# One more pair of convolution taps moved into the attention stage, and a projection that waits for its two operand halves one by one

## What is computed

```
a = rmsnorm(h, g);  z = a @ w_in                    # split into SGU, conv and MLA columns
y_a = spatial gating unit(z_sgu)
y_b = conv module(z_conv):  a * sigmoid(g), causal depthwise convolution of 31 taps over tokens
      (256 channels), layernorm, silu, 256x256 product
y_c = latent attention(c_q, c_kv, k_pe):  8 heads, causal, q and k of 96, v of 64
h  += [norm(y_a) | norm(y_b) | norm(y_c)] @ w_o
h  += two-level mixture of experts(rmsnorm(h))
h  += sigmoid(rmsnorm(h) @ W_g) * rmsnorm(p @ W_p)
```

## Time and profile before

| | |
|---|---|
| three executions | 2377.6, 2371.58, 2376.19 us; median 2376.19 |
| the profiled execution | 2380.11 us, span 2378.4 us from first to last instruction |
| mean granted TensorE clock | 0.956 |
| busy: PE, DVE, ACT, POOL | 2184.1, 1100.9, 594.8, 369.1 us |
| layer 1: front stage, attention stage | to about 288 us, 288 to about 471 us |
| layer 2: front stage, attention stage | about 1207 to 1472 us, 1472 to about 1655 us |

### The profile page before, as it was taken

One profiled execution on the slowest core, in us unless ns is written; L12 is line 12 of the kernel. 1 busy time (PEld: TensorE's weight loads), 2 busy tenths in 40 slices (PEclk: granted clock), 3 DMA queues, 4 the chain that ended last, 5 costly groups with the idle time before them and its releaser, 6 DMA issues.

```text
span 2378.4 us, 32689 instructions
## 1 busy us (share of the span) xinstructions
PE 2184.1 (92%) x8095; PEld 1217.5 (51%) x8095; DVE 1100.9 (46%) x2442; ACT 594.8 (25%) x1325; POOL 369.1 (16%) x545
## 2 busy tenths in 40 slices
PE   5999699999979999978979997999999799999698
PEld 2555477755534444434435554776555344444344
DVE  1488878754411121115425888787535121111253
ACT  2333233422211111111123332443213111111111
POOL 1222100011022222210013221000110222222100
PEclk9999799999889999998989997999998899999799
DMA  6011321001399999955300114210014999999422
GB/s 230 14 27 26 104 92 28 15 27 62 143 319 334 328 318 304 316 181 203 108 27 14 27 26 134 62 41 1 27 62 156 321 320 330 329 314 326 159 94 88
DMA packets 242022, 358.73 MB, mean 151 GB/s; under 512 B 22708, under 2 KB 190980, under 8 KB 241924
## 3 DMA queue, kind: packets, MB, share of 16 engines
q1 hardware_dynamic: 220900, 315.60, 39.7%
q0 software_dynamic: 18720, 33.60, 3.7%
q10 hardware_dynamic: 2304, 8.39, 0.9%
HBM read 324.48 MB, written 67.63 MB: 165 GB/s over the span
## 4 chain that ended last, share of the span: by engine, by line
PE 83%; DVE 6%; issue 5%; DMA 3%; ACT 1%; SPq 1%; DVEq 0%; POOL 0%; ACTq 0%; POOLq 0%
PE ps L1648 32%; PE ps L1957 19%; PE ps L1967 9%; PE ps L1805 4%; PE ps L1835 4%; PE ps L1617 2%; PE ps L1948 2%; PE ps L1819 2%; PE ps L1905 2%; PE ps L1737 2%; DMA h<-in_x_dram 1%; PE ps L1746 1%; DMA region_c<-in_moe_w_up_dram 1%; DVE neg_max L1355 1%; PE ps L1717 1%
## 5 line engine op out<-in xcount | busy, mean ns | idle before, releaser
L1648 PE MATMUL ps<-region_b,region_c 128*128 128x512 f32 x1024 | 453.3, 599 | 2.7 <-DVE region_c L1164 2.7
L1648 PE MATMUL ps<-region_a,region_c 128*128 128x512 f32 (+1 forms) x768 | 325.0, 578 | 14.9 <-ACT region_c L879 14.9
L1957 PE MATMUL ps<-region_c,region_a 128*128 128x512 f32 x704 | 314.4, 600 | 7.7 <-DMA region_c<-in_moe_w_up_dram 6.8
L1648 PEld LDWEIGHTS ps<-region_b,region_c 128*128 128x128 f32 x1024 | 194.1, 193 | 230.1 <-issue 229.6
L1532 DVE SCALAR_TENSOR_TENSOR region_a<-region_a,ps 128x256 f32<-128x256 f32 x65 | 27.4, 421 | 456.5 <-ACT region_a L1052 456.5
L1648 PEld LDWEIGHTS ps<-region_a,region_c 128*128 128x128 f32 x768 | 147.3, 195 | 175.8 <-issue 175.8
L1957 PEld LDWEIGHTS ps<-region_c,region_a 128*128 128x128 f32 x704 | 132.2, 193 | 159.0 <-issue 159.0
L1805 PE MATMUL ps<-region_c 96*128 96x512 f32 (+3 forms) x384 | 160.6, 530 | 0.0
L1967 PE MATMUL ps<-region_c,region_a 128*128 128x512 f32 x352 | 158.4, 593 | 0.7 <-DVE region_c L1539 0.7
L1957 PE MATMUL ps<-region_a 128*128 128x512 f32 x336 | 147.7, 592 | 0.0
L1835 PE MATMUL ps<-region_c,region_a 128*128 128x64 f32 x1152 | 146.8, 274 | 0.0
(11 more groups left out here) (292 smaller groups left out, 2810.3 us busy)
## 6 DMA issues: line engine op xcount, KB each, us to landing
region_c<-in_moe_w_gate_dram SPq DMA_DIRECT2D x44, 1024.0 KB, 9.1
region_c<-in_moe_w_up_dram SPq DMA_DIRECT2D x44, 1024.0 KB, 11.9
region_c<-in_moe_w_down_dram SPq DMA_DIRECT2D x44, 1024.0 KB, 5.7
region_a<-in_moe_w_gate_dram SPq DMA_DIRECT2D x21, 1024.0 KB, 9.7
region_a<-in_moe_w_up_dram SPq DMA_DIRECT2D x21, 1024.0 KB, 12.3
region_a<-in_moe_w_down_dram SPq DMA_DIRECT2D x21, 1024.0 KB, 5.6
region_c<-choice_outputs SPq DMA_DIRECT2D x32, 512.0 KB, 4.4
qk_heads<-gains SPq DMA_DIRECT2D x32, 384.0 KB, 4.2
```

The source lines that it names most:

```text
L1648: ins = mm(dst, lhsT[:, k, :], w[:, k, a:b], start=(k == 0), stop=(k == KD - 1))
L1957: ins = mm(bank(2), xT[:, k, :], w_gu[s][:, k, :], start=(k == 0), stop=(k == KD - 1))
```

## The change

The unit at `TILES - 3`, number 5 (pair 2, channels 128 to 255), is left out of the front stage too, and its taps are done in the attention stage. There the steps j = 0 to 3 of every head now have one tap each, and j = 4 to 7 two each, as before: 12 slots per head and 96 in all, for the 93 taps of the units 5, 6 and 7 in this order. `z_mla` no longer calls `turned`: it waits for the bank and the weights, then for `FX.lo`, issues blocks 0 to 3, waits for `FX.hi`, and issues blocks 4 to 7, with a `settle` behind each wait.

```diff
                 def conv(a, b):
                     def go(t, u, i):
-                        if not (isinstance(t, int) and t >= TILES - 2):
+                        if not (isinstance(t, int) and t >= TILES - 3):
                             taps(t, u, range(a, b))
                     return go
...
-                    if j >= 4:
-
-                        some = range(8 * (hd % 4) + 2 * (j - 4), min(8 * (hd % 4) + 2 * (j - 4) + 2, TAPS))
-                        taps(TILES - 2 + hd // 4, hd // 4, some, acc_last)
+                    first = 12 * hd + j + max(j - 4, 0)
+                    for k in range(first, min(first + 1 + (j >= 4), 3 * TAPS)):
+                        taps(TILES - 3 + k // TAPS, (1 + k // TAPS) % 2, [k % TAPS], acc_last)
...
                 def z_mla(t, u, i):
                     g = TILES * l + t
-                    turned(0, t)
                     pe.wait_ge(*ZM_act.after(g - 1))
                     pe.wait_ge(w_in_loaded[2], 16 * l + 16)
-                    product(bank(4, 0, MLA_IN), aT_mix[u], w_in, 1024, IN).then_inc(*ZM_pe.next("z_mla"))
+                    settle(pe, passed)
+
+                    for steps_, some in ((FX.lo, range(0, 4)), (FX.hi, range(4, KD))):
+                        pe.wait_ge(*steps_.after(24 * l + t))
+                        settle(pe, passed)
+                        for k in some:
+                            ins = mm(bank(4, 0, MLA_IN), aT_mix[u][:, k, :], w_in[:, k, 1024:IN], start=(k == 0), stop=(k == KD - 1))
+                    ins.then_inc(*ZM_pe.next("z_mla"))
```

## The result

| | median | runs | against before |
|---|---|---|---|
| before, same session | 2376.48 us | 2371.58 to 2377.6, four | |
| after | 2340.11 us | 2338.87 to 2340.74, four | 0.9849, 95% interval 0.9834 to 0.9863 |

The changed kernel is 36.4 us faster. Forecast were 21.9. The two profiled executions lie further apart than the medians, 40.8 us in their spans: that of before was 3.6 us above its median.

A forecast was written before the change was run, and what follows sets the result against it. TensorE was taken to bound the front and attention stages, with VectorE close behind in the front stage. 9.1 + 13.8 - 1.0 = 21.9 us saved, taking the median from 2376.2 to 2354.3 us, range 2341 to 2365.

The forecast's parts named there:

- The projection's wait: TensorE's idle time ahead of `z_mla` in front tiles: 0.65 us saved per tile, 14 tiles, 9.1 us.
- rival B: The saving at `z_mla` is given back by a later TensorE wait in the tile; 2363.4 us, chance 0.13.
- VectorE's slack: In a front tile VectorE waits 0.82 us for TensorE; the 0.65 saved fits inside, so TensorE keeps the pace.
- The taps out of the front stage: Between front stage and attention: without unit 5, attention starts 6.9 us earlier per layer, 13.8 us in sum.
- The taps in attention: One new tap per step j = 0 to 3 of attention: about 1.0 us lost, bounds 0 and 24.2 us.
- The clock: TensorE's low clock at the start of attention: up to 6.8 us per layer to be had, none counted.
- My sum: The forecast's total saving over both layers, 21.9 us, with nothing counted for the clock.
- rival A: Clock stays up through the start of attention in one layer or both: 2347.5 or 2340.7 us, chance 0.33.

The follow-up runs named there:

- no_unit5: The changed kernel with the convolution of unit 5 left out altogether, 31 taps and a join less per layer; 2339.31 us, ratio 0.9855.
- unit4: The changed kernel with the taps of unit 4 moved to attention too, two taps in every step there; 2348.45 us, ratio 0.9878.
- gap31: The changed kernel plus 31 unused VectorE taps ahead of the first row maximum of each layer; 2365.06 us, ratio 0.9954.
- gap31_warm8: gap31 plus eight unused `mm` calls (sixteen 512-column matmuls) ahead of the first transposes of each layer; 2354.73 us, ratio 0.9918.
- gap18: The changed kernel plus 18 unused VectorE taps ahead of the first row maximum of each layer; 2351.65 us, ratio 0.9912.
- gap31_warm: gap31 plus five unused `mm` calls (ten 512-column matmuls) ahead of the first transposes of each layer; 2365.78 us, ratio 0.9959.
- gap24: The changed kernel plus 24 unused VectorE taps ahead of the first row maximum of each layer; 2353.35 us, ratio 0.9904.
- split_only: The kernel before with only the new `z_mla` and its split waits, the taps left where they were; 2364.98 us, ratio 0.9955.

## Why the prediction was right, and where it wasn't

**The projection's wait: right.** 0.65 us a tile forecast, 0.70 measured, four tenths of it from the order of the waits, which I had only guessed at between the bounds. No new wait took its place, so rival B is gone. VectorE's slack was read rightly as the limit: its wait of 0.82 us in a tile is 0.19 now.

```profile
199.73 0.69 DVE L1203 SCALAR_TENSOR_TENSOR region_b<-region_b,ps 128x512 f32<-128x512 f32 x1 [0.19 <-ACT region_b L889]
```

By that wait, a further saving of TensorE in the front tile would be worth 0.2 us, and then VectorE would set the pace; no run tried it.

**The taps out of the front stage: right.** 6.9 us per layer forecast, 7.0 measured in layer 1, and the copy of line 974 is what comes late next, as the step said. In layer 2 the same stretch gave 8.45 us, since in the kernel before it held one more low stretch of the clock, worth 1.5 us.

**The taps in attention: right.** 1.0 us forecast, 0.5 per layer in the traces, of which no_unit5 leaves 0.2 to the taps of unit 5 themselves. Reading the slack step by step from the earlier trace rows was worth it: the bound by busy time alone was 24.2 us. unit4 shows that this cost isn't a fixed price per tap: the next 31 took 4.7 us. The waits of VectorE's row maximum for the scores, over heads 1 to 7 of layer 1, show what was used up. In the kernel before, after and in unit4:

```profile
DVE neg_max L1355 <- PE ps L1808: 14.8, 27, 1.2
```

```profile
DVE neg_max L1355 <- PE ps L1813: 5.0, 14, 0.6
```

```profile
DVE neg_max L1360 <- PE ps L1817: 1.7, 3, 0.6
```

The numbers are us in total, how often, and the longest. The first 30 instructions took 9.8 us of these waits, and the next 31 found 5.0 left.

**The clock: wrong.** The step that failed reads "My sum takes none of it, since before the gap the clock had been low too (0.63 over the transition), and since the rows show that the beginning of attention alone doesn't lift it soon." Its size was right: half of 13.57, 6.8 us per layer, against 6.1 and 6.2 measured. The decision to count it at zero was not. Both reasons were misreadings of rows that stood there. Ahead of the earlier trace rows the clock had been low for this stretch (kernel before, TensorE alone):

```profile
271.40:281.60 10.20, 5.91 (x24) 0.50 0.22 58
```

- The 0.63 is a mean over 13.4 us, of the low stretch above and of what follows it. The earlier trace rows show the clock at 0.98 from 281.5 to 285. By my own sum the first exponential would start at 281.03. So the clock would not be up yet, as rival A had it, but about to rise. In the kernel after it rose 1.3 us behind the first exponential in layer 1 and 0.3 us behind it in layer 2. What counts is the clock just behind the moment at which the work would begin, with TensorE at work from there on, and not the mean of the stretch ahead.
- The 17 us at 0.50 show how long it lasts until attention lifts a clock that has fallen. They say nothing of attention on a clock that is up, and the earlier trace rows had 160 us of attention at 1.00. The long low stretch was a consequence of the gap, and so part of its price. gap31 and gap31_warm8 show it: with the gap back, head 0 is 6.1 and 4.1 us longer, and work in the gap gives that back.

With this term the sum is 21.9 + 12.3 = 34.2 us. That it came in full in both layers was not certain even with the gap closed, as layer 2 of unit4 shows. The rule that I had weighed against the rows, in the Trainium skill, "TensorE: Matmul & The Clock Gate", Part 1 (throttled by default, released by sustained activity), gave 35.5, and 36.4 were measured. These runs agree with its outlook, though not with a quick release: in the kernel before, 13.57 us of matmul went by at 0.50 ahead of the rise.

**What else is in the 40.8 us of the spans.** 9.8 for 14 waits, 13.9 for the transition (2 x 6.95), -1.0 for the taps and 12.3 in the two heads make 35.0. The start of layer 2's front stage gave 2.6 and its last iteration 1.5, both low stretches that are gone: 39.1. The remaining 1.7 us lie in the mixture of experts and the last stage, which neither edit touches; I take them for scatter. The medians show 36.4 in place of 40.8 since executions of the kernel before scatter by up to 10 us (2370.04 to 2380.60 in the three sessions) where those of the changed one lie within 3.3. Why, no run here tells. It may also be why the two edits alone add up to 32.6 us by medians, 22.8 + 9.8, and to 41.7 by the spans of the profiled executions, 26.5 + 15.2.

## What to carry to other kernels

When an idle gap of TensorE is to be closed, count the gap and, as what can be had on top, half of the low-clock matmul time behind it (6.8 us here, 6.1 and 6.2 came). Look up the granted clock just behind the moment at which the work would start once the gap is closed, and ask of each low stretch whether the gap made it. The length of the gap alone doesn't give the price. On an engine's queue put waits that are long satisfied ahead of the one that comes last (0.26 us per tile here), and let each part of a product wait for its own part of the input (0.44). Work moved to an engine with slack can be nearly free (0.5 us for 30 instructions) and a little further on no longer (4.7 us for the next 31, where each in full would be 12.1): read the slack place by place.

## What the runs showed of the hardware that was not expected

- The price of an idle time doesn't follow its length. By how much head 0 became longer: 1.3 and 2.0 us with 2.8 us idle (gap18), 4.0 with 3.2 (gap31_warm), 1.8 and 2.1 with 4.8 (gap24), 4.3 in split_only and 6.1 and 6.2 in the kernel before with the same 6.9, and 6.1 and 4.1 with 7.5 (gap31). At the start of layer 2 an idle time under 1 us may decide over some 2.6 us.
- Once low, the clock takes long to come back, and not always equally long: 10.3 us at the end of the front stage of the kernel after, TensorE busy for 6.59 of them; 13.7 us in split_only and 17 in the kernel before at the start of attention, TensorE busy for 13.57 of the 17; 12.8 of 13.6 in layer 2 of unit4; and in gap31, where the gap of 7.5 us came before the rise, 30.7 us in one piece, busy for 19.51. What decides between these was not tried.
